# One output projection computed token tile by token tile, first weight loads and gate sigmoids reordered, in a two-layer hybrid backbone

## The reference

```
u = norm(h)*(1+sc1)+sh1;   p = u @ w_in                     # one input projection
ya = conv_module(p.a)                 # val*sigmoid(gate), depthwise conv of 31 taps, norm, silu
yb = banded_attention(p.q, p.k, p.v)  # 8 heads, sink logits, rotary
yc = mlstm_bidir(...)                 # 4 heads, head norm, output gate
y  = (sig(ga)*(ya@Wa) + sig(gb)*(yb@Wb) + sig(gc)*(yc@Wc)) @ w_out
h  = layer_norm(alpha*h + g1*y)
u2 = h*(1+sc2)+sh2
f  = grouped_moe(u2)                  # 16 experts, router, top group, then top 2 in it
h  = layer_norm(alpha*h + g2*f)
```

## Time and profile before

| | |
|---|---|
| time, three runs | 1720.46, 1723.88, 1725.96 us (median 1723.88) |
| profiled execution | 1721.75 us; span 1719.9 us |
| PE busy | 1597.1 us, 93% of the span |
| DVE, ACT, POOL busy | 45%, 22%, 12% |
| mean granted TensorE clock | 0.977 |
| bytes moved | 360.58 MB, mean 210 GB/s |

### The profile page before, as it was taken

One profiled execution on the slowest core, in us unless ns is written; L12 is line 12 of the kernel. 1 busy time (PEld: TensorE's weight loads), 2 busy tenths in 40 slices (PEclk: granted clock), 3 DMA queues, 4 the chain that ended last, 5 costly groups with the idle time before them and its releaser, 6 DMA issues.

```text
span 1719.9 us, 31380 instructions
## 1 busy us (share of the span) xinstructions
PE 1597.1 (93%) x13022; PEld 977.0 (57%) x13022; DVE 768.9 (45%) x1540; ACT 373.2 (22%) x898; POOL 207.0 (12%) x222
## 2 busy tenths in 40 slices
PE   6899999989999999899999994999989998999994
PEld 2354475455444448765555543777668887555542
DVE  3059924346211012456136655396543114665555
ACT  1101025443100000312222212012643012121211
POOL 0200000000000000014333321000000000343321
PEclk9899999999999999999999998999999999999997
DMA  8633556630141132499679997432102755999994
GB/s 297 191 98 122 195 172 245 227 104 25 54 159 61 50 110 98 154 393 407 229 278 358 405 392 266 143 110 88 56 25 80 255 190 203 346 407 407 407 408 168
DMA packets 172479, 360.58 MB, mean 210 GB/s; under 512 B 13809, under 2 KB 91993, under 8 KB 171827
## 3 DMA queue, kind: packets, MB, share of 16 engines
q1 hardware_dynamic: 162400, 330.43, 52.8%
q0 software_dynamic: 9024, 23.72, 3.9%
q10 hardware_dynamic: 915, 4.42, 0.6%
HBM read 353.58 MB, written 10.35 MB: 212 GB/s over the span
## 4 chain that ended last, share of the span: by engine, by line
PE 67%; issue 14%; DVE 6%; POOL 5%; ACT 4%; DMA 3%; SPq 1%; POOLq 0%; DVEq 0%; ACTq 0%
PE psum L1061 65%; POOL ys L1011 3%; POOL qkT L994 2%; DMA uT<-in_moe_w_gu 1%; PE psum L1159 1%; DMA ring<-in_w_in 1%; DMA ring<-in_w_mod 1%; DVE hstat L2269 1%; ACT arena L1845 1%; ACT arena L1903 1%; PE psum L1335 0%; PE psum L1579 0%; DMA arena<-ys 0%; PE psum L1606 0%; POOL convT L970 0%
## 5 line engine op out<-in xcount | busy, mean ns | idle before, releaser
L1061 PE MATMUL psum<-uT,ring 128*128 128x512 f32 (+1 forms) x1440 | 497.4, 502 | 11.9 <-DMA ring<-in_w_in 7.6
L1061 PEld LDWEIGHTS psum<-uT,ring 128*128 128x128 f32 x1440 | 272.2, 191 | 226.3 <-issue 201.8
L1061 PE MATMUL psum<-ring,mo_tok 128*32 128x256 f32 x4992 | 306.4, 383 | 11.7 <-DVE ring L2572 10.8
L1061 PEld LDWEIGHTS psum<-ring,mo_tok 128*32 128x32 f32 x4992 | 152.7, 110 | 123.2 <-DVE ring L2572 22.4
L1061 PE MATMUL psum<-ring,v_tok 128*32 128x256 f32 x2496 | 152.2, 385 | 0.4 <-ACT v_tok L1971 0.4
L2188 DVE SCALAR_TENSOR_TENSOR convT<-upad,cwT,convT 128x512 f32<-128x512 f32 (+1 forms) x240 | 132.4, 614 | 2.1
L1061 PE MATMUL psum<-ring,uT 128*128 128x256 f32 (+1 forms) x576 | 113.0, 357 | 0.0
L1061 PEld LDWEIGHTS psum<-ring,v_tok 128*32 128x32 f32 x2496 | 76.1, 111 | 60.0 <-issue 15.6
L1061 PEld LDWEIGHTS psum<-ring,uT 128*128 128x128 f32 x576 | 99.3, 190 | 15.5 <-issue 4.2
L2405 DVE TENSOR_TENSOR arena<-psum,mqk 128x512 f32<-128x512 f32 (+1 forms) x16 | 8.9, 558 | 214.0 <-PE psum L1061 214.0
L1061 PE MATMUL psum<-yab,ring 128*128 128x512 f32 (+1 forms) x256 | 88.7, 501 | 5.3 <-ACT mqk L1931 5.3
(11 more groups left out here) (342 smaller groups left out, 1600.0 us busy)
## 6 DMA issues: line engine op xcount, KB each, us to landing
ring<-in_w_in SPq DMA_DIRECT2D x104, 512.0 KB, 4.8
ring<-in_w_mod SPq DMA_DIRECT2D x96, 512.0 KB, 6.6
yab<-in_moe_w_gu SPq DMA_DIRECT2D x51, 512.0 KB
arena<-in_moe_w_gu SPq DMA_DIRECT2D x47, 512.0 KB
uT<-in_moe_w_gu SPq DMA_DIRECT2D x47, 512.0 KB
mv_tok<-in_moe_w_gu SPq DMA_DIRECT2D x26, 512.0 KB
uT<-in_moe_w_dn SPq DMA_DIRECT2D x26, 512.0 KB
mqk<-in_moe_w_gu SPq DMA_DIRECT2D x25, 512.0 KB
```

The costliest lines, as they stand in the source:

```text
L1061: return nc.tensor.matmul(dst, lhsT, rhs, start=start, stop=stop)
```

## The change

Three places change. **Loads:** in SP's list m0 moves ahead of a0, and m1 behind a1. **Gates:** ACT does the three sigmoids of the first gate block ahead of the four copies. **Output product of layer two:** a bank now holds 512 channels of one token tile, so that the first two banks finish tile 0. DVE takes the statistics piece by piece and norms one tile at a time (`norm_tile`); PE transposes tile 0 ahead of the last output bank and tile 1 behind it. The slots of out 0 and out 1 come free with the third bank, those of out 2 and out 3 with the last. Layer one's output product keeps its order. The rest, left out below, is the renaming of semaphore counts.

```diff
@@ -230,9 +230,26 @@
 NORM_TILES = [TT] + [token_tiles(l) for l in range(DEPTH) for which in range(2)]
-def norm_halves(w):
-
-    return sum(NORM_TILES[:w]) // 2
+def norm_tiles(w):
+
+    return sum(NORM_TILES[:w])
+
+
+def norm_steps(w):
+
+    return sum(tiles if x == 2 * DEPTH - 1 else tiles // 2 for x, tiles in enumerate(NORM_TILES[:w]))
+
+
+def out_keys(layer):
+
+    if layer == 0:
+        return [("out", layer, c, h) for h in range(2) for c in range(4)]
+    return [("out", layer, c, t) for t in range(2) for c in range(2)]
+
+
+def out_user(layer, c):
+
+    return ("out", layer, c, 1) if layer == 0 else ("out", layer, c // 2, 1)
 def on_scalar(which, h, k, tiles):
...
@@ -313,9 +330,10 @@
             order += [(b, l, j) for b in ("ya", "yb", "yc_")]
             order += [(b, l, j + GATES_AHEAD[l]) for b in BRANCHES if j + GATES_AHEAD[l] < KD]
         order += [("g1", l, c) for c in range(nt)]
-        order += [("out", l, c, h) for h in range(nt // 2) for c in range(4)]
+        order += out_keys(l) if l == 0 else out_keys(l)[:-1]
         for h in range(nt // 2):
             order += [("tr2", l, h, k) for k in range(KD // 2)]
+            order += [] if l == 0 else out_keys(l)[-1:]
             order += [("nat", l, 0, c) for c in range(2)] if h else []
             order += [("router", l, h)]
         order += [("scores", l)]
...
@@ -714,12 +732,12 @@
                         stream.append((key, spread_ready, spread_before(l) + n_kept))
                     else:
                         used(key, (b, l, 2 * c + 1))
-            for x in MOD_HALVES[0] if l == 0 else []:
+            for x in MOD_HALVES[0] + MOD_HALVES[1][:1] if l == 0 else []:
                 used_modulation(x)
             for c, products in enumerate(BRANCH_A):
                 kind, j = products[-1]
                 used(("a", l, c), (kind, l, j))
-                for x in MOD_HALVES[1][2 * c:2 * c + 2] if l == 0 else []:
+                for x in MOD_HALVES[1][1:] if (l, c) == (0, 1) else []:
                     used_modulation(x)
             used(("v", l), ("v", l))
             used(("kk", l), ("qk", l, 4))
...
@@ -747,7 +765,7 @@
                 if c + l + 1 < KD // 2:
                     used_gates(c + l + 1)
             for c in range(4):
-                used(("out", l, c), ("out", l, c, nt // 2 - 1))
+                used(("out", l, c), out_user(l, c))
             for x in MOD_HALVES[4] if l == 0 else []:
                 used_modulation(x)
             for x in range(NS):
...
@@ -879,7 +897,7 @@
                 elif name == "rows":
                     wait_ready(sp, "modt", len(MOD_GROUPS) - 1)
                 elif l and name in ("arena2", "arena3"):
-                    wait_ready(sp, "out", l, 3, token_tiles(l) // 2 - 1)
+                    wait_ready(sp, *out_keys(l)[-1])
                 else:
                     sp.wait_ge(quads_ready[1], quad_base[l] + 1)
                     for t in range(token_tiles(l)):
...
@@ -1041,7 +1059,7 @@
                 pool.dma_start(wgate[:, :, 0:16], win[l][:, :, C_MG:C_MG + 16]).then_inc(wgate_loaded, 16)
                 pool.wait_ge(hn_ready, l + 1)
                 pool.dma_start(route_row, a["k_route"]).then_inc(route_row_loaded, 16)
-                wait_drained(pool, "out", l, 3, token_tiles(l) // 2 - 1)
+                wait_drained(pool, *out_keys(l)[-1])
                 load_norm_rows(2 * l + 1)
                 dispatch_and_collect(l)
             pool.wait_ge(ln_loaded, 32 * (1 + 2 * DEPTH))
...
@@ -1455,17 +1473,32 @@
                 gate_rows(0, G1)
                 pe.wait_ge(merged_ready, KD * (l + 1))
-                for h in range(nt // 2):
-                    for c in range(4):
-                        if h == 0:
-                            wait_slot(pe, "out", l, c)
-                        w = slot8(slot_of("out", l, c))
-                        wait_bank(pe, "out", l, c, h)
-                        for t in (2 * h, 2 * h + 1):
-                            for k in range(KD):
-                                last = mm(bank("out", l, c, h)[:, (t % 2) * 256:(t % 2 + 1) * 256],
-                                          merged[:, k, t * P:(t + 1) * P], w[:, k, :], k == 0, k == KD - 1)
-                        done(last, "out", l, c, h)
+                def transposes_of_tile(t):
+
+                    pe.wait_ge(h_ready, norm_tiles(2 * l + 1) + t + 1)
+                    for k in range(KD // 2):
+                        key = ("tr2", l, 0, k)
+                        if t == 0:
+                            wait_bank(pe, *key)
+                        for c in range(2):
+                            last = nc.tensor.transpose(bank(*key)[:, (2 * c + t) * P:(2 * c + t + 1) * P],
+                                                       H[:, t, (2 * k + c) * P:(2 * k + c + 1) * P], ident[:, :])
+                        if t:
+                            done(last, *key)
+
+                for key in out_keys(l):
+                    c, part = key[2:]
+                    if key == out_keys(1)[-1]:
+                        transposes_of_tile(0)
+                    wait_bank(pe, *key)
+                    for g in range(2):
+                        x, t = (c, 2 * part + g) if l == 0 else (2 * c + g, part)
+                        wait_slot(pe, "out", l, x)
+                        w = slot8(slot_of("out", l, x))
+                        for k in range(KD):
+                            last = mm(bank(*key)[:, g * 256:(g + 1) * 256], merged[:, k, t * P:(t + 1) * P], w[:, k, :],
+                                      k == 0, k == KD - 1)
+                    done(last, *key)
                 def natural(t):
                     for c in range(2):
@@ -1476,7 +1509,10 @@
                         done(last, "nat", l, t, c)
                 for h in range(nt // 2):
-                    transposes(1, h)
+                    if l == 0:
+                        transposes(1, h)
+                    else:
+                        transposes_of_tile(1)
                     if h:
                         natural(0)
...
@@ -1688,8 +1724,13 @@
             def norm_std(w, h):
-                act.wait_ge(ln_var, norm_halves(w) + h + 1)
+                act.wait_ge(ln_var, norm_steps(w) + h + 1)
                 f(sd[:, 2 * h:2 * h + 2], mv[:, 2 * h:2 * h + 2, 1], ACT.Sqrt, bias=eps[:, :]).then_inc(ln_std, 1)
+
+            def norm_std_of_tile(t):
+
+                act.wait_ge(ln_var, norm_steps(2 * DEPTH - 1) + t + 1)
+                f(sd[:, t:t + 1], mv[:, t:t + 1, 1], ACT.Sqrt, bias=eps[:, :]).then_inc(ln_std, 1)
             act.wait_ge(consts_set, 1)
             norm_std(0, 0)
...
@@ -1740,7 +1781,10 @@
                     w = 2 * l + which
                     tiles = nt if which else TT
-                    if w:
+                    if w == 2 * DEPTH - 1:
+                        for t in range(tiles):
+                            norm_std_of_tile(t)
+                    elif w:
                         norm_std(w, 0)
                     act.wait_ge(folded, w + 2 if w else 1)
                     for h in range(tiles // 2):
...
@@ -1918,12 +1962,12 @@
                 act.wait_ge(hvar, l + 1)
                 f(hstat[:, 2, 0:NH * nt], hstat[:, 1, 0:NH * nt], ACT.Sqrt, bias=eps[:, :], scale=1.0 / MH)\
                     .then_inc(hstd, 1)
-                for h in range(NH):
-                    wait_ready(act, "yc", l, h)
-                    f(yc[:, h, 0:n], bank("yc", l, h)[:, 0:n], ACT.Copy).then_inc(drained_of("yc", l, h), 1)
-
-
-                for j in range(len(SPREAD_GATES[l]) // len(BRANCHES), KD):
+                spread = len(SPREAD_GATES[l]) // len(BRANCHES)
+                for j in range(spread, KD):
+                    if j == spread + 1:
+                        for h in range(NH):
+                            wait_ready(act, "yc", l, h)
+                            f(yc[:, h, 0:n], bank("yc", l, h)[:, 0:n], ACT.Copy).then_inc(drained_of("yc", l, h), 1)
                     if j >= gate_slots(l):
                         wait_drained(act, "yc_", l, j - gate_slots(l))
                     for b, key in enumerate(BRANCHES):
...
@@ -2050,19 +2094,27 @@
                 for t in pair:
                     last = statistics(t)
                 last.then_inc(ln_var, 1)
-                dve.wait_ge(ln_std, norm_halves(w) + h + 1)
+                dve.wait_ge(ln_std, norm_steps(w) + h + 1)
                 link(v.reciprocal(rstd[:, 2 * h:2 * h + 2], sd[:, 2 * h:2 * h + 2]))
                 for t in pair:
                     v.tensor_scalar(H[:, t, :], H[:, t, :], mv[:, t, 0:1], rstd[:, t:t + 1], ALU.subtract, ALU.mult)\
                         .then_inc(h_ready, 1)
+            def norm_tile(t):
+
+                v.bn_aggr(mv[:, t, :], st[:, t, :]).then_inc(ln_var, 1)
+                dve.wait_ge(ln_std, norm_steps(2 * DEPTH - 1) + t + 1)
+                link(v.reciprocal(rstd[:, t:t + 1], sd[:, t:t + 1]))
```

(49 more changed lines are left out.)

2 lines of the change are left out of this document (1 added, 1 removed).

## The result

The changed kernel took 1703.77 us (median of 4 runs, 1700.15 to 1709.38) against 1722.68 (4 runs, 1720.46 to 1725.96): a ratio of 0.9892, 95% interval 0.9859 to 0.9924, so 18.6 us less, with 13 to 24 inside the interval. A second set of pairs, on another chip, gave 1702.36 against 1725.7 us, ratio 0.9859 (0.9842 to 0.9877), some 24 us less. The forecast was 1702 us and 21.5 us of gain. The profiled execution after has a span of 1701.3 us against 1719.9.

A forecast was written before the change was run, and what follows sets the result against it. PE was taken to bound the kernel for two thirds of the chain, transfers setting the end. Loads 9.3, gates 4.7 and 4.3, output product 3.2 sum to 21.5 us: 1702 us forecast, range 1697 to 1710.

The forecast's parts named there:

- The bound: Whole kernel: the chain runs through PE, transfers set the end, and time saved ahead of them reaches the end in full.
- the wait of 7.63: PE ahead of val 2, waiting for a2: the new load order removes this wait, 7.63 us.
- the low clock: The 64 PE records behind the wait for a2: full clock there saves 2.5 us.
- a0: Ahead of val 0: this load comes later in the new order, so PE waits 0 to 0.9 us more, taken as 0.4.
- a3: Ahead of gate 2: this load, issued at about 58 us, makes PE wait 0 to 2.7 us, taken as 0.4.
- Rival 1: Ahead of gate 2: a3 lands at 71 us behind POOL's loads, PE stands 2.7 us; about 1707 us; chance 0.12.
- everything behind moves with it: After the loads: a shift ahead of the last transfer stretch was taken to reach the end in full, 9.3 us.
- rival 3: Gates: no gain, as PE meets ACT's copies at yc, needing copies over 10 us late; 1711 us; chance 0.04.
- the routing chain behind starts from the router and moves with it: Behind layer two's output product: routing shifts with the router, so the 3.2 us gain is kept.
- The inserted transposes: Layer two, ahead of the last output bank: eight transposes add 1.0 us to the chain at full clock.
- Rivals 2 and 4: Last stretch: full link takes back 5.3 us, 1707 to 1708, chance 0.10; or slower transfers, 1733 at 350 GB/s, chance 0.03.
- The price of 5.3 us for four parts: Expert 0's late parts: cost nil with spare link time, 5.3 us at 407 GB/s if that cover were gone.

The follow-up runs named there:

- the filler: The kernel before, with 32 small matmuls on the identity ahead of the wait for a2: ratio 0.9993.
- the second profile: The changed kernel itself, unaltered, run once more for another profile and more pairs: ratio 0.9859.
- the filler ahead of the last transposes: The changed kernel, with 12 small matmuls on the identity ahead of tile 1's transposes in layer two: ratio 0.9869.
- the last version: The changed kernel with POOL's constants behind gate 1 and small matmuls: 16 before tile 1's transposes, 8 in layer one, 4 before the scores: 1701.14 us, ratio 0.9862.

## Why the prediction was right, point by point

**The bound.** Right: what was taken out ahead of the full transfer stretch reached the end. The experts took 233.65 us before, 234.25 after, and 233.7 to 236.1 in all profiles, without order by kernel.

**The loads.** 9.3 forecast, 9.24 measured up to the taps. Of its terms: the wait of 7.63 gone; the low clock 2.5 forecast, 2.6 with the filler; a0 0.4 forecast, 0.24 measured (in three of the seven profiles with the new order ACT was the releaser, and a0 cost nothing); a3 0.4 forecast, 0.78, then 1.58 in the second profile, 0.72 with the loads alone and 0.96 with the filler ahead of the last transposes. Rival 1 named the right cause (POOL's loads ahead of a3, shown by moving them) and overstated its price: PE never waited 2.7 us, and the clock stayed high behind the wait. That everything behind moves with it did not hold in full: in all four profiles with this order and the constants in their old place, 1.5 to 1.9 us were lost again before the head transposes, so that 7.6 of the 9.24 us arrived there in the changed kernel. Why is open, as told below.

**The gates.** 4.7 and 4.3 forecast, 4.78 and 4.36 measured, both gaps and both slow stretches. One reading behind it was wrong and cost nothing: ya and yb together are 16 records and take 7.03 us, not 2 x 7, so the copies, done at 433.2 us, had 5.9 us of cover up to the yc product at 439.0, and rival 3 needed copies only 6 us late. It fell with the kernel that had this edit alone. And the 1.7 to 1.8 us of low clock in layer one cannot be put down to this edit alone: with the loads alone the clock stayed high there behind the full wait (7.11 us), so the edits' shares need not add up. What the prediction did not see is that half the cause would do: without the new order, moving the table load already gives 6.2 of 9.1 us.

**The output product.** 3.2 forecast, 1.83 up to the count. The step that was wrong is "the routing chain behind starts from the router and moves with it". Up to the router's start 4.14 - 0.81 = 3.3 us were gained, but PE had only eight transposes in place of 16 ahead of it and still ran at the low clock, and from the router to the count it took 8.77 instead of 7.27 us. The scores reached DVE 0.5 us later for it, measured from the router's start (4.42 against 3.92 us), and the natural-order transposes and the gate rows stand ahead of the count in PE's own program: DVE had the picks (`r_rank`) ready at 1437.3, PE came to the count at 1438.35. Before, both were there at 1457.4. The inserted transposes cost 0.81, not 1.0 us. The Trainium skill ("TensorE: Matmul & The Clock Gate", "Part 4: PE-mode transpose") has some 275 ns for a bf16 transpose, which as an estimate makes 2.2 us of eight; for these float32 ones the row of 1.04 us for eight decides.

**The sum.** The edits gave 20.2 of the 21.5 us. The missing 1.3 are those of the output product. The rest of the difference to the span's 18.6 comes from the stages between the edits: -1.6, +1.5, +2.2, -3.2, -0.6 us. The last three show no order by kernel. The first two go with an edit, though the prediction had no term for them: the -1.6 with the new order of loads where the constants are in their old place, the +1.5 with the new order of the sigmoids. The +1.5 (276.76 to 275.23 us) is one set of transposes in layer one, behind the same wait of 1.67 us; the kernel before, then the kernel with the gates alone:

```profile
716.21 3.53 PE L1159 MATMUL psum<-ident,H 128*128 128x128 f32 x16 [1.67 <-DVE H L2056]
```

```profile
711.67 1.97 PE L1159 MATMUL psum<-ident,H 128*128 128x128 f32 x16 [1.67 <-DVE H L2056]
```

These transposes took 1.97 us or less in all seven profiles with the new order of sigmoids and 3.33 to 3.55 us in all six without. The -1.6 lies in the attention of layer one, behind the same wait of 2.81 us; the changed kernel, then the last version:

```profile
292.18 1.42 PE L1079 MATMUL psum<-select,upad 128*128 128x16 f32 x8 [2.81 <-DVE yab L2342]
293.53 2.08 PE L1079 MATMUL psum<-qkT 64*128 64x512 f32 x4
```

```profile
291.28 1.03 PE L1080 MATMUL psum<-select,upad 128*128 128x16 f32 x8 [2.81 <-DVE yab L2350]
292.25 1.48 PE L1080 MATMUL psum<-qkT 64*128 64x512 f32 x4
```

Same work and same gap, but the clock falls sooner; 1.0 of the 1.6 us stands in these two rows, the rest in the matmuls behind them (3.65 instead of 3.00 us). That its level makes these differences is read from the rows; why it falls sooner in one kernel than in another is open, as is the part of layer one's expert stage (332.7 to 336.9 us over all profiles).

**Rivals 2 and 4.** The link had room for the late parts, and its full rate stayed at 407 to 408 GB/s. Neither happened. (The price of 5.3 us for four parts is 5.2 by the prediction's own figures.)

## What to carry to other kernels

In an ordered load list, look at whose slot a piece inherits, not only at when it is needed: an idle link ahead of a long wait for a load is the sign. A short wait on the path of a matmul engine can cost twice, once as idle time and once as low clock behind it, so a small part of the wait (here a table load of 1.28 us) may be worth more than its length; the second part does not come every time, and a filler in the wait is no sure means against it (27.7 instead of 30.4 us once, no gain in time from three others). Add such gains up by stage from profiles: single spans moved by 6 us between two executions of one kernel, and stages that nothing touched by 1 to 4.

## What the runs showed that was not expected

A wait cut from 2.85 to 1.43 us, and one from 2.43 to 1.01, were followed by the clock of 2.4 GHz, and so was an uncut one of 2.84 us in one kernel of five, while a gap of 1.67 us was followed by either level in different kernels, behind one of 2.81 us the fall came sooner or later, and gaps of 1.18 and 0.60 us by a fall in one kernel and none in another with the same instructions. A transpose record took 0.12 us at the high level and 0.23 to 0.25 at the low one. And loads issued by POOL delay a load that SP issues 3 us later: with 2.8 MB of POOL's loads around it a3 took 8.6 to 10.6 us to land and was waited for 0.7 to 1.6 us; with 1.8 MB of them moved behind gate 1 (the two rows of the layer norm, 1.0 MB, stayed) it took 4.0 to 5.0 us and was not waited for at all.
